# One-hot gate matrix in bf16, tokens innermost, gates in three bf16 parts

## The chip, the core and the metric

The kernel runs on one core of a Trainium2 chip. The metric is device time in microseconds (us), lower is better; the kernel before took 3196.64 us (median of 3 runs, 3196.23 to 3197.21). Engines are named as in the profile: PE multiplies matrices (PEld is its weight load), DVE is the vector engine, ACT the activation engine, POOL issues the gathers, SP most other DMAs.

## The reference

One decoder block over 512 tokens of width 2048: a mixer (pooling and latent attention), a PEER expert layer, a gated embedding and a final norm, in float32. The change touches only the PEER layer. For each token and each of 8 heads it picks 16 of 128 x 128 experts and gives each a softmax gate:

```python
best_v, best_pos = lax.top_k(cand_v, PEER_TOPK)          # 16 of 256 pairs, per head
expert = jnp.take_along_axis(cand_id, best_pos, axis=-1) # i * 128 + j
gate = jax.nn.softmax(best_v, axis=-1)
hc = einsum('cd,chkd->chk', xc, u[ec]);  ac = gc * gelu(hc);  out = einsum('chk,chkd->cd', ac, v[ec])
```

## The kernel before

For 352 of the tokens the kernel doesn't gather experts. It computes the scores of all 16384 experts with dense products, multiplies them by a gate matrix G that is zero where an expert wasn't picked, and multiplies by all of v. For a token t, G[j, i] is the sum over its 128 picks (8 heads x 16) of gate x onehot(j) x onehot(i). The first 128 of these tokens get G by scattered DMA adds. The other 224 get it from matrix products, and this is the stage that changes, called the one-hot stage below.

The 224 tokens are 7 blocks of 32 (`ONE_TB`), and a block is 4 groups of 8 tokens (`OH`): 28 groups. The picks lie on the 128 partitions. Per group:

- DVE compares the numbers i and j of the picks with the row 0..127 (`iota`) and gets `one_ij`, 2 x 8 x 128 float32 (L1713), then multiplies the one-hot of i by the gate and gets `one_g`, 8 x 128 float32 (L1717). The number 0..127 is innermost in both. The buffers alternate, so group q waits for the products of group q-2.
- PE multiplies, per token, the one-hot of j (stationary, 128 x 128) with `one_g` (moving, 128 columns): 8 products in float32 into two PSUM banks (L828). The profile has two records for each float32 product, 16 in a group.
- ACT copies both banks into `g_blk`, with the tokens innermost there (L1196). After 4 groups SP stores the block.

Between the groups PE does a dense product of its own, with weights that are split into a high and a low part: unit by unit, each in 4 quarters of 12 matmuls (L533 to L535, 352 columns, float32r). The order on PE in a block is quarter, group, quarter, group, and so on. ACT makes the high part of the next unit's weights in two halves (`w_hi`, L949), between the copies of a block's first, second and third group. DVE makes the low part (`w_lo`, L1350) from it: the half 0 after the one-hots of the second group, the half 1 after those of the third. SP loads the next weights once a half of `w_lo` is done. DVE also takes dot products with gathered rows (`row_dot`, L1689): two in block 0, one behind each of the blocks 1, 2 and 4. POOL issues the gathers and waits for these.

Ahead of the stage, PE turns the picked i, j and gates into token columns, ACT copies them to `hk_t` (L1171), and then ACT issues 8 small DMAs and goes on with the next weights.

Of the kernel before, what the change touches and what calls it, by code (L numbers as in the profile page):

```python
# [8 lines left out]
BF16 = mybir.dt.bfloat16  # L9
U32 = mybir.dt.uint32  # L10
I32 = mybir.dt.int32
ALU = mybir.AluOpType
ACT = mybir.ActivationFunctionType
AX = mybir.AxisListType

P = 128
# [12 lines left out]
NK = 128  # L29
HK = PH * TOPK  # L30
TD = 352
TCD = TD // P + 1
# [41 lines left out]
OH = 8  # L74
# [10 lines left out]
def build_block(nc, x_t, p_t, positions, gains, consts, rope_cols, pool_inv, w_in, pool_w, w_head, w_v,  # L85
                w_o, w_q, keys, u_t, u_rows, v, w_proj, w_gate, out_t):
    ctx = ExitStack()
    with ctx:
# [4 lines left out]
        def at(name, offset, shape, dtype=F32):  # L93
            return nc.alloc_sbuf_tensor_at(name, shape, dtype, offset=base + offset)

        K = 1024
# [5 lines left out]
        h_at, one, two, rest = 40 * K, 72 * K, 136 * K, 200 * K  # L102
# [10 lines left out]
        iota = at("iota", rest + 512, [P, P])  # L113
# [73 lines left out]
        b_inv = at("b_inv", one + 52 * K + 320, [P, TC])  # L187
        t_if = [at(f"t_if{i}", one + 53 * K + 256 * i, [P, TC, TOPK]) for i in range(2)]

        hk_t = at("hk_t", one, [P, 3, TCD * P])  # L190
        one_ij = [at(f"one_ij{i}", one + (6 + 8 * i) * K, [P, 2, OH, NK]) for i in range(2)]
        one_g = [at(f"one_g{i}", one + (22 + 4 * i) * K, [P, OH, NK]) for i in range(2)]
        g_blk = [at(f"g_blk{i}", one + (30 + 16 * i) * K, [P, NK, TB]) for i in range(2)]

        h_out = at("h_out", one + 62 * K, [P, TD])
# [25 lines left out]
        bank = [ctx.enter_context(nc.psum_tensor(f"bank{i}", [P, T], F32)) for i in range(8)]  # L221

        def sem(name):
            return ctx.enter_context(nc.semaphore(name))
# [70 lines left out]
        gates_put = sem("gates_put")  # L295
        hk_turned = sem("hk_turned")
        hk_ready = sem("hk_ready")
        oh_g = sem("oh_g")
        oh_ij = sem("oh_ij")
        g_done = sem("g_done")  # L300
# [59 lines left out]
        def row_loads(k):  # L360

            return k // 2 + 1 if k < EARLY else (k - EARLY) // 4 + 1 + (EARLY // 2 if k % 4 < 2 else 0)
# [167 lines left out]
        def _(pe):  # L530
# [280 lines left out]
            for i in range(3):  # L811
                for t in range(1, TCD):
                    mm = pe.transpose(bank[i][:, t * P:(t + 1) * P],
                                      sel[i][:, t, :, :].rearrange("p h k -> p (h k)"), ident[:, :])
# [4 lines left out]
            def g_group(q, s, first=False):  # L819

                pe.wait_ge(oh_g, q + 1)
                for half in range(2):
                    out = bank[6 + half]
                    if not first:
                        pe.wait_ge(g_out, 2 * q - 1 + half)
                    for t in range(4):
                        o = 4 * half + t
                        mm = pe.matmul(out[:, t * P:(t + 1) * P], one_ij[s][:, 1, o, :], one_g[s][:, o, :],  # L828
                                       start=True, stop=True)
                    mm.then_inc(g_done, 1)  # L830

            def g_block(b, k):
# [82 lines left out]
            for n in range(DC):  # L915
# [7 lines left out]
                for c in range(2):  # L923
                    mm = passes(bank[n % 4][:, :], b + c, u % 2, pt_hi[:, c, :], pt_lo[:, c, :], c == 0, c == 1)
# [17 lines left out]
        def _(act):  # L942
# [206 lines left out]
            for e in range(ALONE):  # L1149
                hi(U_ALONE + e + 1, (U_ALONE + e + 1) % 2)  # L1150
                if e < 2:
                    rows_stage(4 * e)
                    rows_stage(4 * e + 1)
                if e == 2:
                    act.wait_ge(col_made, 1)
                    act.activation(rinv_col[:, :], bank[2][:, 0:4], ACT.Copy).then_inc(col_made, 1)
                if e == 3:
                    gates(PH - 1)
                spill(2 * (PH - 1) + e, e % 2, U_ALONE + e)
                if e < 2:  # L1160
                    rows_stage(4 * e + 2)
                    rows_stage(4 * e + 3)
                    rows_evict(2 * e)
                    rows_evict(2 * e + 1)
                if e == 1:
                    act.activation(stage[0][:, 0, :].rearrange("p (q t) -> p q t", t=TK),
                                   rinv[:, TD:TD + TK].unsqueeze(1).to_broadcast([P, 4, TK]), ACT.Copy).then_inc(stage_ready, 1)
                if e == 5:
                    for i in range(3):
                        act.wait_ge(hk_turned, i + 1)  # L1170
                        act.activation(hk_t[:, i, P:TCD * P], bank[i][:, P:TCD * P], ACT.Copy).then_inc(hk_ready, 1)  # L1171
                    act.wait_ge(topk_step, PER_TOPK * PH)
                    for q in range(4):
                        ts = slice(TK * q, TK * (q + 1))
                        act.dma_start(expert_b[ts, :], expert_c[P - TK:P, 2 * q:2 * q + 2, :].rearrange("p a k -> p (a k)"))\
                           .then_inc(expert_b_in, 16)
                        act.dma_start(gate_rows_b[ts, :],
                                      sel[2][P - TK:P, TCD - 1, 2 * q:2 * q + 2, :].rearrange("p a k -> p (a k)"))\
                           .then_inc(expert_b_in, 16)
# [165 lines left out]
        def _(dve):  # L1345
            def lo(u, slot, halves=(0, 1), n=8):

                for s in halves:
                    dve.wait_ge(hi_ready, 2 * u + s + 1)
                    dve.tensor_tensor(w_lo[slot][:, 8 * s:8 * s + n, :], raw[s][:, 0:n, :],  # L1350
                                      w_hi[slot][:, 8 * s:8 * s + n, :].bitcast(F32), ALU.subtract)\
                       .then_inc(lo_ready, 1)
# [333 lines left out]
            def row_dot(k, b, loads, part_b=False):  # L1686

                dve.wait_ge(row_in[b], 16 * loads)
                dve.scalar_tensor_tensor(row[b][:, :], row[b][:, :], 1.0, (x_rows_b if part_b else x_rows)[:, :],  # L1689
                                         ALU.mult, ALU.mult,  # L1690
                                         accum_out=column(dots_b if part_b else dots, k)).then_inc(row_done, 1)
# [9 lines left out]
            dve.wait_ge(rows_out, 4)  # L1701
            for k in range(2):
                row_dot(k, k % 2, row_loads(k))
            for n in range(6):
                lo(U_ALONE + 7 + n, (U_ALONE + 1 + n) % 2)
                for k in ((2,), (3, 4), (5,), (6, 7), (8,), (9, 10))[n]:
                    row_dot(k, k % 2, row_loads(k))

            def one_hots(q, s, first=False):
                o = [P, 2, OH, NK]  # L1710
                if not first:
                    dve.wait_ge(g_done, 2 * q - 2)
                dve.tensor_tensor(one_ij[s][:, :, :, :], iota[:, None, None, :].to_broadcast(o),  # L1713
                                  hk_t[:, 0:2, bass.ds(OH * q + P, OH)].unsqueeze(3).to_broadcast(o), ALU.is_equal)\
                   .then_inc(oh_ij, 1)
                dve.wait_ge(oh_ij, q + 1)
                dve.tensor_tensor(one_g[s][:, :, :], one_ij[s][:, 0, :, :],  # L1717
                                  hk_t[:, 2, bass.ds(OH * q + P, OH)].unsqueeze(2).to_broadcast([P, OH, NK]), ALU.mult)\
                   .then_inc(oh_g, 1)

            dve.wait_ge(hk_ready, 3)

            BLOCK_DOT = {1: 13, 2: 14, 4: 15}

# [447 lines left out]
```

## Time and profile before

| | us |
|---|---|
| median of 3 runs | 3196.64 |
| the profiled execution | 3193.13 |
| its span | 3190.9 |
| PE busy | 3069.8 |
| DVE busy | 2493.5 |
| ACT busy | 1053.9 |

The profile is one execution. "Busy" is the time in which an engine has an instruction in work. A busy PE isn't at its peak, as the ends of matmuls are modelled; the distance from one start to the next shows its pace. A line such as L828 is that of the kernel before.

### The profile page before, as it was taken

To read this page: it belongs to the slowest core of one execution; us is meant where nothing else is said; L and a number is where in the kernel's file an instruction comes from. 1 tells how busy PE (TensorE), PEld (TensorE's weight loads), DVE (VectorE), ACT (ScalarE), POOL (GpSimd) and SP (SyncE) were. 2 spreads that over 40 slices of the span, in tenths; PEclk is the share of its full clock that TensorE was granted. 3 is DMA by queue.
4 is the path that set the end of the run, shared out by engine and by line. 5 is a ranking of instruction groups with operands and counts; after the bars stand their busy time and mean duration, and the time that the engine had idled before them with its cause. 6 is when DMAs were issued, how large, how long until landed. Compare 5 with 4: busy or idle time off the path is not lost.

```text
span 3190.9 us, 47109 instructions
## 1 busy us (share of the span) xinstructions
PE 3069.8 (96%) x17044; PEld 2843.0 (89%) x17044; DVE 2493.5 (78%) x3559; ACT 1053.9 (33%) x1409; POOL 815.3 (26%) x530
## 2 busy tenths in 40 slices
PE   7999999999998879999999999999999999999997
PEld 5777778788888779999999999999999999999775
DVE  6444444499996979999999998999999999966545
ACT  4223433222233543333333333333333333324322
POOL 3030000046675112222222223232323232302000
PEclk8999999999999999999999999999999999999998
DMA  3233222344558669999999998999999999953222
GB/s 142 93 135 115 79 80 92 105 112 105 114 146 275 221 255 336 358 346 337 348 334 350 333 352 319 340 344 339 344 337 348 335 351 339 346 188 113 93 92 92
DMA packets 254755, 756.37 MB, mean 237 GB/s; under 512 B 37216, under 2 KB 90976, under 8 KB 210656
## 3 DMA queue, kind: packets, MB, share of 16 engines
q1 hardware_dynamic: 185184, 414.05, 38.0%
q0 software_dynamic: 64512, 335.64, 28.0%
q10 hardware_dynamic: 4992, 5.80, 0.5%
q8 instruction: 41, 0.67, 0.1%
q14 instruction: 26, 0.21, 0.0%
HBM read 722.28 MB, written 33.10 MB: 237 GB/s over the span
## 4 chain that ended last, share of the span: by engine, by line
PE 76%; DVE 16%; DMA 3%; issue 3%; ACT 1%; POOL 1%; DVEq 0%; ACTq 0%; SPq 0%; POOLq 0%
PE bank L533 24%; PE bank L535 24%; PE bank L534 23%; DVE w_lo L1350 3%; DVE row L1689 2%; DVE one_ij L1713 1%; DMA raw<-in_v 1%; PE bank L625 1%; PE bank L648 1%; PE bank L626 1%; DVE w_lo L1362 1%; DMA row<-in_u_rows,expert 1%; DVE one_g L1717 1%; DVE x_lo L1870 1%; PE bank L828 1%
## 5 line engine op out<-in xcount | busy, mean ns | idle before, releaser
L533 PE MATMUL bank<-x_hi,w_hi 128*128 128x352 f32 (+1 forms) x3024 | 1073.8, 355 | 30.9 <-DVE x_lo L1378 16.6
L535 PE MATMUL bank<-x_hi,w_lo 128*128 128x352 f32 (+1 forms) x3024 | 1063.7, 352 | 0.0
L534 PE MATMUL bank<-x_lo,w_hi 128*128 128x352 f32 (+1 forms) x3024 | 1057.6, 350 | 0.0
L533 PE MATMUL bank<-a_hi,w_hi 128*128 128x352 f32 x2048 | 664.8, 325 | 11.6 <-DVE a_lo L1764 8.2
L534 PE MATMUL bank<-a_lo,w_hi 128*128 128x352 f32 x2048 | 664.1, 324 | 0.0
L535 PE MATMUL bank<-a_hi,w_lo 128*128 128x352 f32 x2048 | 664.1, 324 | 0.0
L533 PEld LDWEIGHTS bank<-x_hi,w_hi 128*128 128x128 f32 x3024 | 573.4, 190 | 86.1 <-DVE w_lo L1350 16.8
L535 PEld LDWEIGHTS bank<-x_hi,w_lo 128*128 128x128 f32 x3024 | 573.4, 190 | 44.0
L534 PEld LDWEIGHTS bank<-x_lo,w_hi 128*128 128x128 f32 x3024 | 573.8, 190 | 43.1 <-issue 1.2
L533 PEld LDWEIGHTS bank<-a_hi,w_hi 128*128 128x128 f32 x2048 | 387.6, 189 | 14.1 <-DVE a_lo L1764 7.3
L534 PEld LDWEIGHTS bank<-a_lo,w_hi 128*128 128x128 f32 x2048 | 387.7, 189 | 0.0
L535 PEld LDWEIGHTS bank<-a_hi,w_lo 128*128 128x128 f32 x2048 | 387.7, 189 | 0.0
L961 ACT ACTIVATE w_hi<-raw 128x1024 fp32r<-128x1024 f32 x216 | 223.1, 1053 | 435.2 <-PE bank L535 424.2
L961 ACT ACTIVATE w_hi<-raw_b 128x1024 fp32r<-128x1024 f32 x216 | 223.3, 1053 | 418.5 <-PE bank L535 410.0
L2050 POOL DMA_INDIRECT row<-in_v,expert x128 | 231.9, 1812 | 476.5 <-DVE x_rows L1698 391.7
L2050 POOL DMA_INDIRECT row<-in_u_rows,expert x128 | 200.0, 1563 | 586.8 <-DVE row L1689 534.4
L1350 DVE TENSOR_TENSOR w_lo<-raw,w_hi 128x1024 fp32r<-128x1024 f32 (+1 forms) x236 | 278.6, 1213 | 80.8 <-ACT w_hi L949 74.6
L1838 DVE TENSOR_TENSOR h<-bank,h 128x352 f32<-128x352 f32 x512 | 257.0, 517 | 83.8 <-PE bank L535 83.7
L2032 POOL DMA_INDIRECT gate_matrix<-put_gate,cell x128 | 229.3, 1791 | 358.8 <-DVE cell L1647 300.8
L1698 DVE SCALAR_TENSOR_TENSOR x_rows<-row,mix,x_rows 128x2048 f32<-128x2048 f32 x128 | 299.9, 2343 | 6.6 <-DMA row<-in_v,expert 6.6
L949 ACT ACTIVATE w_hi<-raw 128x1024 fp32r<-128x1024 f32 (+1 forms) x236 | 235.9, 1031 | 201.7 <-PE bank L535 67.0
L1689 DVE SCALAR_TENSOR_TENSOR row<-row,x_rows 128x2048 f32<-128x2048 f32 x128 | 292.0, 2282 | 8.6 <-DMA row<-in_u_rows,expert 8.6
(221 smaller groups left out, 2894.8 us busy)
## 6 DMA issues: line engine op xcount, KB each, us to landing
raw<-in_u_t SPq DMA_DIRECT2D x164, 512.0 KB
raw<-in_v SPq DMA_DIRECT2D x132, 512.0 KB
raw_b<-in_v SPq DMA_DIRECT2D x124, 512.0 KB
raw_b<-in_u_t SPq DMA_DIRECT2D x92, 512.0 KB
g_tile<-gate_matrix SPq DMA_DIRECT2D x32, 704.0 KB
raw<-in_w_o SPq DMA_DIRECT2D x32, 512.0 KB
raw<-in_w_q SPq DMA_DIRECT2D x32, 512.0 KB
raw<-in_w_gate SPq DMA_DIRECT2D x32, 512.0 KB
```

Of the source, the lines that this page charges most:

```text
L533: pe.matmul(out, w_hi[slot][:, blk, :], m_hi, start=first, stop=False)
L534: pe.matmul(out, w_hi[slot][:, blk, :], m_lo, start=False, stop=False)
L535: return pe.matmul(out, w_lo[slot][:, blk, :], m_hi, start=False, stop=last)
L625: pe.matmul(out[:, 0:n], q_n[:, ts], k_n[:, 0:n], start=True, stop=False)
L949: act.activation(w_hi[slot][:, 8 * s:8 * s + n, :], raw[s][:, 0:n, :], ACT.Copy)\
L961: act.activation(w_hi[slot][:, 8 * s:8 * s + 8, :], raw_two[x][s][:, :, :], ACT.Copy).then_inc(hi_ready, 1)
L1350: dve.tensor_tensor(w_lo[slot][:, 8 * s:8 * s + n, :], raw[s][:, 0:n, :], w_hi[slot][:, 8 * s:8 * s + n, :].bitcast(F32), ALU.subtract)\
L1689: dve.scalar_tensor_tensor(row[b][:, :], row[b][:, :], 1.0, (x_rows_b if part_b else x_rows)[:, :], ALU.mult, ALU.mult, accum_out=column(d ...
L1698: dve.scalar_tensor_tensor(to[:, :], row[b][:, :], column(mix_b if part_b else mix, k), to[:, :], ALU.mult, ALU.add).then_inc(row_done, 1)
L1838: dve.tensor_tensor(hc, bank[2 + c][:, 0:TD], hc, ALU.add).then_inc(v_added, 1)
L2032: pool.indirect_dma_start(g_dram.rearrange("b j i t -> (b j i t)").unsqueeze(1), bass.IndirectOffsetOnAxis(ap=cell[:, hd, k:k + 1], axis=0 ...
L2050: pool.indirect_dma_start(row[b][:, :], None, table, bass.IndirectOffsetOnAxis(ap=index, axis=0))\
```

## The change

`hk_t` becomes three tensors: i and j in bf16 (`hk_ij`), the gate in float32 (`hk_gate`) and the gate in three bf16 parts (`hk_g`). ACT writes the first part and also a bf16 table `iota_oh` of 128 x 8 numbers, in which each number stands 8 times. DVE takes each part from the gate and rounds the rest to the next part (`split_gates`), ahead of the fourth of six weight units. `one_ij` and `one_g` are bf16 with the 8 tokens innermost, and `one_g` has three parts: 3 x 128 x 8 elements. Each product per token becomes three bf16 products into the same place, and both operands of a product are read at a step of 8 elements, 16 bytes. The numbers 0 to 127 and the ones are exact in bf16.

```diff
--- before.py
+++ after.py
@@ -187,9 +187,12 @@
         b_inv = at("b_inv", one + 52 * K + 320, [P, TC])
         t_if = [at(f"t_if{i}", one + 53 * K + 256 * i, [P, TC, TOPK]) for i in range(2)]
 
-        hk_t = at("hk_t", one, [P, 3, TCD * P])
-        one_ij = [at(f"one_ij{i}", one + (6 + 8 * i) * K, [P, 2, OH, NK]) for i in range(2)]
-        one_g = [at(f"one_g{i}", one + (22 + 4 * i) * K, [P, OH, NK]) for i in range(2)]
+        hk_ij = at("hk_ij", one, [P, 2, TCD * P], BF16)
+        hk_g = at("hk_g", one + 2 * K, [P, 3, TCD * P], BF16)
+        hk_gate = at("hk_gate", one + 28 * K, [P, TCD * P])
+        one_ij = [at(f"one_ij{i}", one + (6 + 4 * i) * K, [P, 2, NK, OH], BF16) for i in range(2)]
+        one_g = [at(f"one_g{i}", one + (14 + 6 * i) * K, [P, 3, NK, OH], BF16) for i in range(2)]
+        iota_oh = at("iota_oh", one + 26 * K, [P, NK, OH], BF16)
         g_blk = [at(f"g_blk{i}", one + (30 + 16 * i) * K, [P, NK, TB]) for i in range(2)]
 
         h_out = at("h_out", one + 62 * K, [P, TD])
@@ -295,6 +298,7 @@
         gates_put = sem("gates_put")
         hk_turned = sem("hk_turned")
         hk_ready = sem("hk_ready")
+        hk_split = sem("hk_split")
         oh_g = sem("oh_g")
         oh_ij = sem("oh_ij")
         g_done = sem("g_done")
@@ -825,8 +829,9 @@
                         pe.wait_ge(g_out, 2 * q - 1 + half)
                     for t in range(4):
                         o = 4 * half + t
-                        mm = pe.matmul(out[:, t * P:(t + 1) * P], one_ij[s][:, 1, o, :], one_g[s][:, o, :],
-                                       start=True, stop=True)
+                        for part in range(3):
+                            mm = pe.matmul(out[:, t * P:(t + 1) * P], one_ij[s][:, 1, :, o], one_g[s][:, part, :, o],
+                                           start=part == 0, stop=part == 2)
                     mm.then_inc(g_done, 1)
 
             def g_block(b, k):
@@ -1168,7 +1173,11 @@
                 if e == 5:
                     for i in range(3):
                         act.wait_ge(hk_turned, i + 1)
-                        act.activation(hk_t[:, i, P:TCD * P], bank[i][:, P:TCD * P], ACT.Copy).then_inc(hk_ready, 1)
+                        act.activation(hk_ij[:, i, P:TCD * P] if i < 2 else hk_gate[:, P:TCD * P], bank[i][:, P:TCD * P],
+                                       ACT.Copy).then_inc(hk_ready, 1)
+                    act.activation(hk_g[:, 0, P:TCD * P], bank[2][:, P:TCD * P], ACT.Copy).then_inc(hk_ready, 1)
+                    act.activation(iota_oh[:, :, :], iota[:, :].unsqueeze(2).to_broadcast([P, NK, OH]), ACT.Copy)\
+                       .then_inc(hk_ready, 1)
                     act.wait_ge(topk_step, PER_TOPK * PH)
                     for q in range(4):
                         ts = slice(TK * q, TK * (q + 1))
@@ -1701,24 +1710,36 @@
             dve.wait_ge(rows_out, 4)
             for k in range(2):
                 row_dot(k, k % 2, row_loads(k))
+
+            def split_gates():
+
+                rest_of = hk_gate[:, P:TCD * P]
+                dve.wait_ge(hk_ready, 4)
+                for part in range(2):
+                    dve.tensor_tensor(rest_of, rest_of, hk_g[:, part, P:TCD * P], ALU.subtract).then_inc(hk_split, 1)
+                    dve.wait_ge(hk_split, 2 * part + 1)
+                    dve.tensor_copy(hk_g[:, part + 1, P:TCD * P], rest_of).then_inc(hk_split, 1)
+                    dve.wait_ge(hk_split, 2 * part + 2)
+
             for n in range(6):
+                if n == 3:
+                    split_gates()
                 lo(U_ALONE + 7 + n, (U_ALONE + 1 + n) % 2)
                 for k in ((2,), (3, 4), (5,), (6, 7), (8,), (9, 10))[n]:
                     row_dot(k, k % 2, row_loads(k))
 
             def one_hots(q, s, first=False):
-                o = [P, 2, OH, NK]
+                o, o3 = [P, 2, NK, OH], [P, 3, NK, OH]
+                ts = bass.ds(OH * q + P, OH)
                 if not first:
                     dve.wait_ge(g_done, 2 * q - 2)
-                dve.tensor_tensor(one_ij[s][:, :, :, :], iota[:, None, None, :].to_broadcast(o),
-                                  hk_t[:, 0:2, bass.ds(OH * q + P, OH)].unsqueeze(3).to_broadcast(o), ALU.is_equal)\
-                   .then_inc(oh_ij, 1)
+                dve.tensor_tensor(one_ij[s][:, :, :, :], iota_oh[:, None, :, :].to_broadcast(o),
+                                  hk_ij[:, :, ts].unsqueeze(2).to_broadcast(o), ALU.is_equal).then_inc(oh_ij, 1)
                 dve.wait_ge(oh_ij, q + 1)
-                dve.tensor_tensor(one_g[s][:, :, :], one_ij[s][:, 0, :, :],
-                                  hk_t[:, 2, bass.ds(OH * q + P, OH)].unsqueeze(2).to_broadcast([P, OH, NK]), ALU.mult)\
-                   .then_inc(oh_g, 1)
-
-            dve.wait_ge(hk_ready, 3)
+                dve.tensor_tensor(one_g[s][:, :, :, :], one_ij[s][:, 0:1, :, :].to_broadcast(o3),
+                                  hk_g[:, :, ts].unsqueeze(2).to_broadcast(o3), ALU.mult).then_inc(oh_g, 1)
+
+            dve.wait_ge(hk_ready, 5)
 
             BLOCK_DOT = {1: 13, 2: 14, 4: 15}
```

## Rows read from the trace of the kernel before

**Rows 1.** The page: span, and busy time of the engines.

```profile
span 3190.9 us, 47109 instructions
...
PE 3069.8 (96%) x17044; PEld 2843.0 (89%) x17044; DVE 2493.5 (78%) x3559; ACT 1053.9 (33%) x1409; POOL 815.3 (26%) x530
```

**Rows 2.** The chain that ended last, into the one-hot stage: start us, us, what.

```profile
974.32 1.24 DVE w_lo L1350
...
1027.75 3.79 PE bank L828 x16
```

**Rows 3.** Groups, 1024 to 1160 us: xcount | busy us, mean ns | idle before, releaser.

```profile
L1713 DVE TENSOR_TENSOR one_ij<-iota,hk_t 128x2048 f32<-128x2048 f32 x28 | 64.0, 2286 | 0.0
L828 PE MATMUL bank<-one_g,one_ij 128*128 128x128 f32 x448 | 58.1, 284 | 29.7 <-DVE one_g L1717 29.7
L1196 ACT ACTIVATE g_blk<-bank 128x512 f32<-128x512 f32 x56 | 57.4, 1122 | 61.7 <-PE bank L828 61.7
...
L1717 DVE TENSOR_TENSOR one_g<-one_ij,hk_t 128x1024 f32<-128x1024 f32 x28 | 34.3, 1225 | 1.0
```

**Rows 4.** Busy time of each engine in one block, with the granted clock.

```profile
1072.00:1091.00 19.00, 15.62 (x112) 14.75 (x112) 18.10 (x13) 10.18 (x12) 2.77 (x1) 1.00 0.59 218
```

**Rows 5.** DVE in order of time: start us, us, what [idle before].

```profile
1088.10 1.23 DVE L1717 TENSOR_TENSOR one_g<-one_ij,hk_t 128x1024 f32<-128x1024 f32 x1
...
1093.57 1.23 DVE L1350 TENSOR_TENSOR w_lo<-raw,w_hi 128x1024 fp32r<-128x1024 f32 x1 [0.78 <-ACT w_hi L949]
```

**Rows 6.** PE in order of time, blocks 2 to 6: start us, us, what.

```profile
1070.28 2.05 PE L828 MATMUL bank<-one_g,one_ij 128*128 128x128 f32 x16 [1.74 <-DVE one_g L1717]
...
1089.46 2.05 PE L828 MATMUL bank<-one_g,one_ij 128*128 128x128 f32 x16 [1.66 <-DVE one_g L1717]
...
1106.84 1.95 PE L828 MATMUL bank<-one_g,one_ij 128*128 128x128 f32 x16
...
1108.54 0.41 PE L533 MATMUL bank<-x_hi,w_hi 128*128 128x352 f32 x1
...
1110.60 1.95 PE L828 MATMUL bank<-one_g,one_ij 128*128 128x128 f32 x16
...
1156.72 2.05 PE L828 MATMUL bank<-one_g,one_ij 128*128 128x128 f32 x16 [0.56 <-DVE one_g L1717]
```

**Rows 7.** PE in order of time, matmuls of 512 and 352 columns.

```profile
253.61 0.40 PE L533 MATMUL bank<-l_hi,w_hi 128*128 128x512 f32 x1
...
257.72 0.39 PE L533 MATMUL bank<-l_hi,w_hi 128*128 128x512 f32 x1
...
1095.60 0.33 PE L533 MATMUL bank<-x_hi,w_hi 128*128 128x352 f32 x1
...
1096.58 0.33 PE L533 MATMUL bank<-x_hi,w_hi 128*128 128x352 f32 x1
```

**Rows 8.** Groups of the whole span: a strided read, a dense read, dense writes.

```profile
L1386 DVE TENSOR_REDUCE fold<-ident 128x32 f32<-128x128 f32 x1 | 0.4, 367 | 0.0
...
L1621 DVE TENSOR_REDUCE b_sum<-b_exp 128x4 f32<-128x64 f32 x8 | 1.8, 220 | 0.3
...
L1018 ACT ACTIVATE q_n<-bank 128x512 f32<-128x512 f32 x12 | 7.2, 598 | 6.7 <-PE bank L535 6.6
...
L1109 ACT ACTIVATE h_out<-bank 128x352 f32<-128x352 f32 x32 | 14.8, 461 | 58.0 <-PE bank L535 55.2 <-DMA spilled_scores<-h_out 2.8
```

**Rows 9.** Groups of the whole span: DVE with two tensor operands and with one.

```profile
L1408 DVE TENSOR_TENSOR ang<-ang,turn 128x512 f32<-128x512 f32 x1 | 0.7, 691 | 0.0
...
L1402 DVE TENSOR_SCALAR turn<-ang 128x512 f32<-128x512 f32 x1 | 0.4, 428 | 0.0
```

**Rows 10.** ACT and DVE in order of time, ahead of the stage.

```profile
973.23 2.00 ACT L949 ACTIVATE w_hi<-raw 128x1024 fp32r<-128x1024 f32 x2 [5.03 <-issue]
...
989.66 2.35 DVE L1350 TENSOR_TENSOR w_lo<-raw,w_hi 128x1024 fp32r<-128x1024 f32 x2
995.29 2.29 DVE L1689 SCALAR_TENSOR_TENSOR row<-row,x_rows 128x2048 f32<-128x2048 f32 x1 [3.27 <-DMA row<-in_u_rows,expert]
```

## The prediction

> **What bounds the kernel now.** I read the page first: PE is busy 3069.8 of 3190.9 us [rows 1], so nearly everything elsewhere hides behind PE, and a change counts only where PE waits or where PE's own work grows. The chain of waits enters the one-hot stage through DVE's weight split and leaves DVE at the first group of products, at 1027.75 us [rows 2]; from there it runs over DVE's one-hots in every block. The groups of the stretch say the same: between 1024 and 1160 us PE is idle 29.7 us ahead of its products, all of it for `one_g`, while ACT is idle 61.7 us for PE [rows 3]. DVE is busy 18.10 of 19 us in a block, PE 15.62, at full granted clock (2.4 GHz) [rows 4]. The last group starts at 1156.72 us and takes 2.05 [rows 6], so the stage, from the first product to the last, is 1158.77 - 1027.75 = 131.0 us.
>
> PE's own part: the group that starts at 1106.84 is followed by a dense quarter at 1108.54 and that by a group at 1110.60 [rows 6]. So a group is 1.70 us of PE and a quarter 2.06, together 3.76, 15.0 for a block of four. A block takes 1106.84 - 1089.46 = 17.4 us without a row dot and 1089.46 - 1070.28 = 19.2 with one [rows 6]. The 2 to 4 us between are what DVE costs, and all that the change can save there.
>
> **DVE's one-hots.** 1024 elements take 1.225 us and 2048 take 2.286 [rows 3]: 1.036 ns each and 0.164 fixed. Now `one_ij` has 2048 and `one_g` 3072 elements. At the old pace per element that is 2.29 + 3.35 us; at two elements a cycle 1.22 + 1.75. The trace has no bf16 operation with two tensors. It has DVE at twice its pace with one tensor: 512 elements take 0.428 us, against 0.691 with two [rows 9]. So the bounds of a group are 2.97 and 5.64 us, against 3.51 now. I take 2.97: all operands are 16 bits wide and dense innermost. The Trainium skill, VectorE: DVE Perf Modes, "The perf-mode tier table", gives a bf16 `tensor_tensor` from SBUF twice the rate; no run here shows it yet, and the value taken agrees with it.
>
> **PE's products.** This is the term that decides. There are 24 bf16 matmuls of 128 columns in a group in place of 16 float32 records in 1.70 us. If the reads don't matter, their pace comes from the dense rows: 18 steps of 512 columns in 257.72 - 253.61 = 4.11 us are 228 ns each, 6 steps of 352 in 0.98 us are 163 ns [rows 7]. That is 0.406 ns a column (one a cycle of 2.4 GHz) and 20 ns fixed, so 72 ns at 128 columns and 24 x 72 = 1.73 us a group: no saving on PE, and no loss.
>
> But both operands are now read at a step of 16 bytes, where before their elements were neighbours. Two rows show an access with such a jump. ACT's copy into `g_blk` writes 512 elements at a jump of 128 bytes: 57.4 / 56 = 1.025 us, against 0.598 for a dense write of as many [rows 3, 8]. Dense, 352 elements take 0.461, so an element is 0.137 / 160 = 0.86 ns and 0.16 is fixed, and the strided write costs (1.025 - 0.16) / 512 = 1.69 ns an element, twice as much. DVE's `fold` reads 128 elements at a jump of 128 bytes in 0.367 us; a dense reduction of 64 takes 0.220, of which 64 x 1.036 ns are work and 0.154 fixed, so the strided read costs (0.367 - 0.154) / 128 = 1.67 ns an element [rows 8]. Two engines whose dense paces differ (0.86 and 1.04 ns) pay the same 1.67 ns per jump: that looks like the memory, not the engine. If PE pays it too, a matmul of 128 columns takes 128 x 1.67 = 213 ns, and a group 24 x 213 = 5.12 us. Dense float32r reading at one column a cycle needs 16 bytes in 1.67 ns, so nothing in the trace shows PE reaching more of the memory than that. The bounds of a group on PE are then 1.3 us (24 x 128 columns at 2.4 GHz, nothing fixed) and 5.6 (the 20 ns added to 213). I take 5.12, by the two rows with a jump.
>
> The Trainium skill, Advanced Engine Details and Errata, "SBUF Cachelines", speaks against the layout too: lines of 16 bytes, and at least two hits on a line are needed to absorb the access latency. A step of 16 bytes gives one hit. The two rows agree that jumps cost. The page states no price for PE. The Trainium skill's other page on it, SBUF — State Buffer, "Door 1: The DMA port swizzle", calls a stride of 8 bf16 elements free; by that the sum would be that of the first rival, and the rows as they stand speak against it.
>
> **The sum.** With 5.12 us a group, PE is the bound of the stage: 4 x (5.12 + 2.06) = 28.7 us a block, while DVE needs 4 x 2.97 + 2 x 1.23 = 14.3 (24 even at the slow bound) and ACT 10.2 as now [rows 4]. PE never waits after the first group, so the stage is 28 x 5.12 + 27 x 2.06 = 143.4 + 55.6 = 199.0 us, against 131.0: +68.0. The idle time of 29.7 us is swallowed by this. The five row dots and `w_lo` hide behind PE.
>
> Ahead of the stage ACT gets two more instructions in front of its 8 DMA issues and of the `w_hi` at 973.23 [rows 10]: a copy of 256 elements from PSUM (about 0.27 us behind another) and `iota_oh`, 1024 elements, about 1.0. DVE waits for that `w_hi` and its `w_lo` at 974.32 is in the chain [rows 2], so +1.2. The four DVE steps of `split_gates`, 256 elements each, are at most 4 x (0.164 + 0.267) = 1.7 us, ahead of the `w_lo` at 989.66. DVE then waits 3.27 us for a gathered row [rows 10], which covers them; what isn't covered is the weight load that this `w_lo` releases, so 0 to 1.7, and I take 0.5. The first one-hots are 0.5 shorter. Together +1.2, between -0.5 and +3.
>
> Behind the stage the last copies, the store of `gate_matrix` and the wait for it are as before: 0.
>
> Total +68.0 + 1.2 = +69. The profiled execution has 3193.13 us, its span of 3190.9 and 2.2 around it; that gives 3262. It lies 3.5 us under the median of the runs, so against the median the forecast is 3196.64 + 69 = 3266 us. With 233 ns a matmul it is 28 x 5.59 + 55.6 = 212, +82, 3279.
>
> **Rival 1: PE reads at full pace, faster.** For it: before, nothing is strided on PE, so no row shows a price there; one line holds what eight bf16 columns need if it is kept. Against it: the two rows with jumps. Then a group is 1.73 us on PE and DVE's order decides. From the start of a block's first group to the first `w_lo` there are 1093.57 - 1089.46 = 4.1 us (products, copies, `w_hi`) [rows 5, 6]; then `w_lo` 1.15, one-hots 2.94, `w_lo` 1.14, one-hots 2.94: the fourth group starts at 12.3. Its products and a quarter (1.73 + 2.06) bring the next block to 16.1, against 17.4; with a row dot, one-hots (2.94) and dot (2.2) behind 12.3 give 17.4, against 19.2. Three blocks save 1.3, three 1.8, block 0 about 2: 11.3. Less 1.2 ahead: -10, 3186 us; 3184 at 56 ns a matmul.
>
> **Rival 2: PE reads at half pace.** A price of one cycle of 1.2 GHz per jump is 107 ns a matmul. For it: PE takes two columns in that time when dense, so its port may be wider than DVE's. A group is 2.56 us, the stage 28 x 2.56 + 55.6 = 127.3, less than 131.0: -3.7 + 1.2 = -2.5, 3194 us. With the fixed 20 ns it is 3.05 a group, 141.0, +11, 3208. The point from which this turns slower is 2.7 us a group.
>
> **Rival 3: PE's clock falls as well.** With products at a quarter of their pace PE streams less, and the clock does fall here: behind the idle wait ahead of the stage the first group took 3.79 us, the later ones about 2 [rows 2, 6]. If it fell to 1.2 GHz through the stage, each quarter would take 4.1: 27 x 2.06 = 55 more, 3321 us. Against it: the dense quarters still stream 2.06 us of every 7.2.
>
> **Rival 4: DVE doesn't pair elements**, with PE at full pace. 5.6 us a group: a block is 4 x 5.55 + 2.3 = 24.5, the stage 7 x 24.5 + 11 for the dots = 182, about +50: 3247 us. Against it: the operands are dense and 16 bits wide, and DVE does pair elements with one tensor [rows 9].
>
> **How the numbers follow.** Chances: forecast (PE at 213 to 233 ns) 0.44, rival 1 0.25, rival 2 0.22, rival 3 0.05, rival 4 0.04. A difference under 0.2% (6.4 us) can't be told from none. Faster is rival 1 but for its edge, 0.23. The same are that edge and over half of rival 2, 0.14. Slower is the rest, 0.63. For 8 in 10 the range must take in rival 1, rival 2 and the forecast with its higher pace: 3184 to 3285. The forecast's own range is 3258 to 3285.
>
> **What would show it.** Right: the start of a bf16 matmul in the products lies 200 to 235 ns behind the one before; a block is about 29 us; PE has no idle time for `one_g` after the first group and DVE has plenty. `one_ij` takes 1.22 us and `one_g` 1.75 (wrong if 2.3 and 3.3). The first product starts 0 to 3 us after 1027.75. Wrong: matmuls 55 to 80 ns apart with blocks of 16 to 17 us (rival 1), or 107 to 130 apart with blocks of 18 to 20 (rival 2); a granted clock of about 0.5 in the stage (rival 3).

## The result, and the profile after

The changed kernel took 3315.88 us (median of 4 runs, 3310.97 to 3316.97), the kernel before 3196.93 us on the same chip (3196.23 to 3201.55). The ratio is 1.037, with a 95% interval of 1.0354 to 1.0385: it is slower by 119 us. The forecast was 3266 us with a range to 3285. The sign and the place were right, and 50 us were missing.

The page of the kernel after, its span, the busy time of the engines, and the clock granted to PE in 40 slices of the span. It answers to [rows 1].

```profile
span 3314.7 us, 47564 instructions
...
PE 3211.4 (97%) x17268; PEld 2928.2 (88%) x17268; DVE 2482.6 (75%) x3563; ACT 1059.4 (32%) x1411; POOL 809.1 (24%) x530
...
PEclk9999999999997677999999999999999999999998
```

The span grew by 3314.7 - 3190.9 = 123.8 us and PE's busy time by 141.6. DVE's fell by 11. The four slices of 7, 6, 7 and 7 are the one-hot stage. Before, all slices but the first and the last had 9.

Groups of the stage after, 1028 to 1280 us, columns as in [rows 3]:

```profile
L833 PE MATMUL bank<-one_g,one_ij 128*128 128x128 bf16 x672 | 162.8, 415 | 9.5 <-DVE one_g L1739 9.5
...
L1739 DVE TENSOR_TENSOR one_g<-one_ij,hk_g 128x3072 bf16<-128x3072 bf16 x28 | 49.2, 1759 | 1.0
...
L1736 DVE TENSOR_TENSOR one_ij<-iota_oh,hk_ij 128x2048 bf16<-128x2048 bf16 x28 | 34.2, 1222 | 43.1 <-PE bank L833 43.1
...
L1359 DVE TENSOR_TENSOR w_lo<-raw,w_hi 128x1024 fp32r<-128x1024 f32 x14 | 17.2, 1226 | 84.4 <-ACT w_hi L954 84.4
```

Set beside [rows 3], the roles have changed. DVE's two operations fell from 2286 + 1225 ns to 1222 + 1759 = 2981 ns a group, and DVE is now idle ahead of `one_ij` (43.1 us) and of its weight split (84.4 us). PE waited 29.7 us for `one_g` before, 8.6 of it ahead of the first group. It now waits 9.5, all of it ahead of the first group. Its products went from 58.1 to 162.8 us of busy time.

Three stretches of the stage after. Columns: start:end and length in us, busy us (and instructions) of PE, PEld, DVE, ACT and POOL, granted PE clock, share of the DMA engines, GB/s. They answer to [rows 4].

```profile
1066.00:1102.00 36.00, 36.00 (x145) 27.13 (x144) 16.16 (x13) 10.96 (x11) 0.99 (x1) 0.64 0.31 117
1102.00:1137.00 35.00, 35.00 (x145) 26.27 (x144) 16.06 (x13) 10.91 (x11) 1.97 (x1) 0.74 0.32 123
1173.00:1209.00 36.00, 36.00 (x145) 27.11 (x144) 16.41 (x13) 11.05 (x11) 4.15 (x3) 0.69 0.33 119
```

A block now takes 35 to 36 us of PE without a gap, where 17.4 to 19.2 went by before and the prediction had 28.7. PE is busy 36.00 of 36 us and yet has only 0.64 of its full clock.

PE in order of time, in the kernel after: start us, us, what.

```profile
1030.94 5.81 PE L833 MATMUL bank<-one_g,one_ij 128*128 128x128 bf16 x24 [9.53 <-DVE one_g L1739]
...
1084.97 5.82 PE L833 MATMUL bank<-one_g,one_ij 128*128 128x128 bf16 x24
1090.43 0.66 PE L537 MATMUL bank<-x_hi,w_hi 128*128 128x352 f32 x1
1090.89 0.49 PE L538 MATMUL bank<-x_lo,w_hi 128*128 128x352 f32 x1
1091.18 0.49 PE L539 MATMUL bank<-x_hi,w_lo 128*128 128x352 f32 x1
...
1094.12 5.84 PE L833 MATMUL bank<-one_g,one_ij 128*128 128x128 bf16 x24
...
1272.75 5.81 PE L833 MATMUL bank<-one_g,one_ij 128*128 128x128 bf16 x24
1283.35 0.47 PE L539 MATMUL bank<-x_hi,w_lo 128*128 128x352 f32 x1
1283.64 0.34 PE L537 MATMUL bank<-x_hi,w_hi 128*128 128x352 f32 x1
```

Two sizes are to be read here. A group holds PE from 1084.97 to 1090.43: 5.46 us, which is 227 ns for each of 24 matmuls in the mean. The quarter behind it, the same float32r matmuls as before, starts them 1091.18 - 1090.89 = 0.29 us apart, where the rows before had 0.163. For 352 columns that is 1.2 GHz in place of 2.4, and this quarter takes 1094.12 - 1090.43 = 3.69 us. At the end one sees the clock come back: at 1283.64 us, 5.1 us after the last group ended, a matmul's record falls from 0.49 to 0.34.

Where the 123.8 us are, from these rows. From the first product to the end of the last the stage takes 1278.56 - 1030.94 = 247.6 us (1278.56 is the end of the last group's record, 1272.75 + 5.81), against 131.0: +116.6. In it:
- groups: 28 x (5.46 - 1.70) = +105.3;
- quarters: (247.6 - 28 x 5.46) / 27 = 3.51 us in the mean in place of 2.06, so 27 x 1.45 = +39.2;
- PE's idle time and its first group at a low clock, in the stage before: -(131.0 - 28 x 1.70 - 27 x 2.06) = -27.8.

The first product starts 3.2 us later (1030.94 against 1027.75), and what follows the stage takes 4.0 us more. 116.6 + 3.2 + 4.0 = 123.8.

### The profile page after: what moved, and what is told of

Same layout as the page of the kernel before. It is cut to its first block, busy times and chain, and to the rows that moved or that the text cites. A ratio compares the mean times of both kernels' runs of the same rounds, so it can differ in the third digit from the quotient of the medians.

```text
span 3314.7 us, 47564 instructions
## 1 busy us (share of the span) xinstructions
PE 3211.4 (97%) x17268; PEld 2928.2 (88%) x17268; DVE 2482.6 (75%) x3563; ACT 1059.4 (32%) x1411; POOL 809.1 (24%) x530
## 4 chain that ended last, share of the span: by engine, by line
PE 80%; DVE 13%; DMA 3%; issue 2%; ACT 1%; DVEq 0%; ACTq 0%; POOL 0%; SPq 0%; POOLq 0%
PE bank L537 24%; PE bank L539 24%; PE bank L538 23%; PE bank L833 5%; DVE w_lo L1359 2%; DVE row L1698 1%; DMA raw<-in_v 1%; PE bank L629 1%; DMA raw<-in_u_t 1%; PE bank L652 1%; PE bank L630 1%; DVE w_lo L1371 1%; DVE x_lo L1891 1%; DVE x_lo L1387 1%; DVE h L1859 1%
## 5 line engine op out<-in xcount | busy, mean ns | idle before, releaser
L537 PE MATMUL bank<-x_hi,w_hi 128*128 128x352 f32 (+1 forms) x3024 | 1092.3, 361 | 34.6 <-DVE x_lo L1387 19.2
L539 PE MATMUL bank<-x_hi,w_lo 128*128 128x352 f32 (+1 forms) x3024 | 1079.5, 357 | 0.0
L538 PE MATMUL bank<-x_lo,w_hi 128*128 128x352 f32 (+1 forms) x3024 | 1073.7, 355 | 0.0
L537 PEld LDWEIGHTS bank<-x_hi,w_hi 128*128 128x128 f32 x3024 | 587.8, 194 | 90.9 <-DVE w_lo L1359 18.6
L539 PEld LDWEIGHTS bank<-x_hi,w_lo 128*128 128x128 f32 x3024 | 586.9, 194 | 43.9
L538 PEld LDWEIGHTS bank<-x_lo,w_hi 128*128 128x128 f32 x3024 | 587.5, 194 | 43.0 <-issue 1.2
```

The source lines that it names most:

```text
L537: pe.matmul(out, w_hi[slot][:, blk, :], m_hi, start=first, stop=False)
L538: pe.matmul(out, w_hi[slot][:, blk, :], m_lo, start=False, stop=False)
L539: return pe.matmul(out, w_lo[slot][:, blk, :], m_hi, start=False, stop=last)
```

## Experiments

The forecast's theory was that PE pays for every 16-byte line that an operand's read touches, by a price of the memory. After the result there were four questions. Is it the step of the reads? Which of the two operands? Is the lower clock due to it as well, or to the bf16 matmuls as such? And is DVE's saving to be had without PE's loss?

### Dense reads on PE, all else as changed

```diff
+ij_flat = one_ij[s][:, 1, :, :].rearrange("p n o -> p (n o)")
 for part in range(3):
-    mm = pe.matmul(out[:, t * P:(t + 1) * P], one_ij[s][:, 1, :, o], one_g[s][:, part, :, o],
+    g_flat = one_g[s][:, part, :, :].rearrange("p n o -> p (n o)")
+    mm = pe.matmul(out[:, t * P:(t + 1) * P], ij_flat[:, o * P:(o + 1) * P], g_flat[:, o * P:(o + 1) * P],
...
```

> The changed kernel, but each bf16 product reads both operands as 128 neighbouring elements of the same tiles (the values are others, so the gate matrix is left wrong). DVE, ACT and the counts are untouched. Theory (the 16-byte step sets PE's pace, and the slow products let the clock fall): matmuls 72 ns apart (55 to 80), 1.73 us a group, granted clock 1.0 in the stage, blocks of 16 to 17.5 us, total 3189 us (3183 to 3195), so slightly faster than before or the same. Rival (the three-fold count of bf16 products is the cost, not the step): matmuls stay near 227 ns apart and the time near 3316. Second rival (the clock falls for another reason): products 72 to 110 ns apart but quarters still 3.5 us, total about 3230.

This kernel leaves the gate matrix wrong. It took 3187.01 us (9 runs, 3177.92 to 3190.26), a ratio to the kernel before of 0.9963 [0.995, 0.9976]. The same stage, in PE's order of time and as a window:

```profile
1049.36 1.51 PE L835 MATMUL bank<-one_g,one_ij 128*128 128x128 bf16 x24 [2.73 <-DVE one_g L1741]
1050.68 0.41 PE L537 MATMUL bank<-x_hi,w_hi 128*128 128x352 f32 x1
```

```profile
1060.00:1090.00 30.00, 23.74 (x248) 22.15 (x249) 28.75 (x22) 16.80 (x19) 3.43 (x2) 1.00 0.63 238
```

The same 672 matmuls, the same bytes in the tiles and the same work on DVE; only the step is 1 element in place of 8. A group takes 1.32 us (55 ns a matmul) in place of 5.46, the clock is 1.00, and 129 us are gone. So the whole loss, PE's pace and the clock, comes from the strided reads. This is the kernel that the prediction's first rival described (3186 us), with the pace that it lacked.

### Four steps side by side

The eight token pairs of a group read both operands at 1, 2, 4 and 8 elements (2, 4, 8 and 16 bytes), two pairs each.

```diff
+def at_step(flat, k):
+    first = o % k + (o // k) * P * k
+    return flat[:, first:first + P * k - k + 1:k] if k > 1 else flat[:, first:first + P]
...
+if o in (0, 1):
+    mm = pe.matmul(to, at_step(ij_flat, 1), at_step(g_flat, 1), **ends)
+elif o in (2, 3):
+    mm = pe.matmul(to, at_step(ij_flat, 2), at_step(g_flat, 2), **ends)
...
```

> The changed kernel, but within each group of 8 tokens the first two are read by PE at a step of 1 element in both operands, the next two at 2, then 4, then 8 (other values, so the gate matrix is left wrong). Theory A (each 16-byte line costs 1.67 ns whatever is taken from it): per matmul 72 ns at step 1, 60 to 72 at step 2, 107 to 125 at step 4, 227 at step 8. Theory B (a cliff: only a step of a whole line costs): 72, 72, 72, 227. A group is 2.9 us by A, 2.7 by B; total 3200 to 3225 depending on the clock.

One run, 3204.09 us. One group; the four lines are the four steps, six matmuls each:

```profile
1082.08 0.51 PE L843 MATMUL bank<-one_g,one_ij 128*128 128x128 bf16 x6
1082.42 0.51 PE L845 MATMUL bank<-one_g,one_ij 128*128 128x128 bf16 x6
1082.77 0.88 PE L847 MATMUL bank<-one_g,one_ij 128*128 128x128 bf16 x6
1083.46 1.58 PE L849 MATMUL bank<-one_g,one_ij 128*128 128x128 bf16 x6
1084.68 0.53 PE L537 MATMUL bank<-x_hi,w_hi 128*128 128x352 f32 x1
```

From start to start six matmuls take 0.34, 0.35, 0.69 and 1.22 us: 57, 58, 115 and 203 ns each. The last figure is low, because the dense matmul behind a strided stretch starts before the last strided one has had its full share; a whole group of 24 at that step gave 227. Steps of 1 and 2 elements cost the same, 4 elements cost twice that, 8 elements four times. So each 16-byte line costs about 1.8 ns (64 lines in 115 ns, 128 in 227), and where a line holds enough columns the one column a cycle of 2.4 GHz is the limit. No step above 8 elements was run, so that the price stays at one line's there isn't shown for PE. The Trainium skill, Advanced Engine Details and Errata, "SBUF Cachelines", says that at least two hits on a line are needed to absorb the latency. For PE's bf16 operands two aren't enough in this run: with two hits (step 4) a matmul takes 115 ns against 57 dense, and with four (step 2) 58.

### Which operand

```diff
+if o in (0, 1):
+    mm = pe.matmul(to, at_step(ij_flat, 1), at_step(g_flat, 8), **ends)
+elif o in (2, 3):
+    mm = pe.matmul(to, at_step(ij_flat, 8), at_step(g_flat, 1), **ends)
...
```

The other two quarters of the pairs read both dense, and both at 8.

> The changed kernel, but within each group of 8 tokens two are read with only the moving operand at a step of 8 elements, two with only the stationary, two with both dense, two with both at a step of 8 (other values, so the gate matrix is left wrong). Theory: the moving operand sets the pace: 227, 72, 72, 227 ns a matmul. Rival: the weight load pays too and isn't hidden: 227, 150 to 230, 72, and 227 or more. If the two add up, both strided would be slower than moving alone.

One run, 3219.10 us. One group, in that order:

```profile
1087.78 1.53 PE L843 MATMUL bank<-one_g,one_ij 128*128 128x128 bf16 x6
1089.13 0.55 PE L845 MATMUL bank<-one_g,one_ij 128*128 128x128 bf16 x6
1089.52 0.50 PE L847 MATMUL bank<-one_g,one_ij 128*128 128x128 bf16 x6
1089.85 1.55 PE L849 MATMUL bank<-one_g,one_ij 128*128 128x128 bf16 x6
1091.04 0.52 PE L537 MATMUL bank<-x_hi,w_hi 128*128 128x352 f32 x1
```

```profile
1090.00:1130.00 40.00, 40.00 (x264) 31.17 (x263) 28.13 (x21) 20.50 (x21) 1.70 (x1) 1.00 0.50 191
```

A strided moving operand (`one_g`, in the second place here) takes 1.35 us for six, 225 ns each. A strided stationary operand (`one_ij`, the weight load) takes 0.39 us, 65 ns, against 55 with both dense. So the moving operand sets nearly the whole price, and the weight load at the same step costs 10 ns. The theory had 72 ns for each of the two.

This bears on the prediction's reason. The strided weight load touches the same 128 lines, and it keeps up with a matmul every 65 ns: 0.5 ns a line at most. So 1.7 ns isn't what the memory asks of every reader. On PE it belongs to the read of the moving operand.

The window has PE reading half of its products at the slow pace, busy throughout, with the clock at 1.00. It isn't so in the whole stage. A window and PE's order of time further on:

```profile
1130.00:1180.00 50.00, 50.00 (x323) 39.10 (x323) 33.98 (x26) 24.83 (x25) 6.42 (x3) 0.97 0.44 162
```

```profile
1156.35 0.66 PE L537 MATMUL bank<-x_hi,w_hi 128*128 128x352 f32 x1
...
1160.03 1.53 PE L843 MATMUL bank<-one_g,one_ij 128*128 128x128 bf16 x6
```

One quarter, from 1156.35 to 1160.03 us, ran at 1.2 GHz and took 3.68 us, with no idle time of PE ahead of it.

### One product in place of three

This kernel leaves out two of the three bf16 parts of each gate.

```diff
-for part in range(3):
-    mm = pe.matmul(out[:, t * P:(t + 1) * P], one_ij[s][:, 1, :, o], one_g[s][:, part, :, o],
-                   start=part == 0, stop=part == 2)
+mm = pe.matmul(out[:, t * P:(t + 1) * P], one_ij[s][:, 1, :, o], one_g[s][:, 0, :, o],
+               start=True, stop=True)
```

> The changed kernel with only the first of the three bf16 products per token (two thirds of the products left out, so gates are rounded), operands still at a step of 8 elements: 8 slow matmuls in a group, 8 x 227 ns = 1.82 us. Theory (the clock falls because slow products fill over half of PE's time): here they fill under half, the granted clock stays near 1.0 and the quarters at 2.06 us; total 3190 (3185 to 3200). Rival (strided products lower the clock however few they are): quarters 3.5 us, 28 x 1.82 + 27 x 3.5 = 145 us for the stage, total about 3214.

3191.26 us (8 runs), ratio 0.9982 [0.9971, 0.9992]. Two windows of its stage:

```profile
1049.00:1066.00 17.00, 16.59 (x74) 13.73 (x73) 12.02 (x10) 8.70 (x10) 0.00 (x0) 0.77 0.51 193
1084.00:1101.00 17.00, 16.48 (x85) 12.96 (x84) 15.56 (x13) 10.88 (x12) 1.70 (x1) 1.00 0.73 258
```

PE in order of time, a group at the low clock and one at the full clock:

```profile
1051.58 2.08 PE L832 MATMUL bank<-one_g,one_ij 128*128 128x128 bf16 x8
1053.29 0.66 PE L537 MATMUL bank<-x_hi,w_hi 128*128 128x352 f32 x1
...
1056.90 2.06 PE L832 MATMUL bank<-one_g,one_ij 128*128 128x128 bf16 x8
1058.60 0.53 PE L537 MATMUL bank<-x_hi,w_hi 128*128 128x352 f32 x1
```

Eight strided matmuls take 1.71 us of PE at the low clock and 1.70 at the full one, as long as the 16 float32 records did [rows 6]. So the low clock doesn't slow the strided reads; it slows the dense quarters, here to 3.61 us (1056.90 - 1053.29). And 16 more strided matmuls, as in the changed kernel's group, cost 5.46 - 1.71 = 3.75 us, 234 ns each: that is their pace from start to start, and 227 is the mean of a group, whose last matmul holds up the dense one behind it by less.

The total came as the theory had it, the clock only in part. Of seven windows of 17 or 18 us over the stage two have 1.00, three 0.91 and the first two 0.78 and 0.77. Nor does the time in strided reads order the runs: the run before had more of it, 1.35 + 1.19 us of each group and quarter of about 5.4, against 1.7 of about 3.9 here, and behind the first groups it lost its clock in one quarter only. What brings the fall isn't settled by these two.

### As much PE time, but dense

Is the clock lower because of the strided reads, or because a group of bf16 matmuls lasts over 5 us? This kernel computes every dense product four times over.

```diff
-for part in range(3):
+for part in (0, 1, 2) * 4:
```

> Dense reads as in e1_dense, with each of the 24 products of a group issued four times (other values): 96 dense matmuls of 57 ns are 5.4 us a group, as long as the 24 strided ones. Theory (the clock falls because PE streams few columns while it reads at a step): here PE streams all the time, the granted clock stays at 1.0, quarters take 2.06 us, the stage is 28 x 5.4 + 27 x 2.06 = 207 us, total 3276 us (3268 to 3284), 40 us under the changed kernel. Rival (the clock falls because of long bf16 groups between float32r quarters, whatever their reads): quarters 3.5 us, total 3316.

3286.30 us (2 runs), ratio 1.0273 [1.0255, 1.0292]. PE in order of time, and a window:

```profile
1080.41 5.53 PE L835 MATMUL bank<-one_g,one_ij 128*128 128x128 bf16 x96
1085.75 0.41 PE L537 MATMUL bank<-x_hi,w_hi 128*128 128x352 f32 x1
...
1087.81 5.53 PE L835 MATMUL bank<-one_g,one_ij 128*128 128x128 bf16 x96
...
1155.59 0.42 PE L537 MATMUL bank<-x_hi,w_hi 128*128 128x352 f32 x1 [2.99 <-issue]
...
1162.73 7.97 PE L835 MATMUL bank<-one_g,one_ij 128*128 128x128 bf16 x96 [4.92 <-issue]
```

```profile
1060.00:1090.00 30.00, 30.00 (x442) 29.46 (x440) 16.56 (x13) 10.90 (x11) 1.73 (x1) 1.00 0.34 120
```

A group takes 5.34 us, within 2% of the 5.46 of the changed kernel, and the quarter behind it 2.06 (1087.81 - 1085.75), with the clock at 1.00. So it is the strided reading, not the length or the kind of the groups, that takes the clock. Whether the clock follows the jumps themselves or only the slow pace that they give PE, no run separates: this one changes both. The kernel is 30 us faster than the changed one, although its groups take nearly as long: that difference is the quarters at the lower clock. It is some 10 us over the 3276 that were expected, and the last two rows hold these: two stops of PE with no releaser, 2.99 and 4.92 us, and one group of 7.97 us in place of 5.53, 10.3 in all. Why PE stopped there isn't known. The other execution (3284.24 us) is over the 3276 too, by 8 us, so something of the kind may belong to this kernel; that execution has no profile.

### Two tokens innermost

PE pays nothing for a step of 2 elements, and DVE may need no more than two neighbours innermost. So the tiles get the two tokens of a pair innermost, in place of eight. Nothing is left out.

```diff
-one_ij = [at(f"one_ij{i}", one + (6 + 4 * i) * K, [P, 2, NK, OH], BF16) for i in range(2)]
-one_g = [at(f"one_g{i}", one + (14 + 6 * i) * K, [P, 3, NK, OH], BF16) for i in range(2)]
+one_ij = [at(f"one_ij{i}", one + (6 + 4 * i) * K, [P, OH // 2, 2, NK, 2], BF16) for i in range(2)]
+one_g = [at(f"one_g{i}", one + (14 + 6 * i) * K, [P, OH // 2, 3, NK, 2], BF16) for i in range(2)]
...
-mm = pe.matmul(out[:, t * P:(t + 1) * P], one_ij[s][:, 1, :, o], one_g[s][:, part, :, o],
+mm = pe.matmul(out[:, t * P:(t + 1) * P], one_ij[s][:, o // 2, 1, :, o % 2],
+               one_g[s][:, o // 2, part, :, o % 2],
...
```

`hk_ij`, `hk_g` and `iota_oh` get the same order, and with them the instructions that write and read them.

> The changed kernel with two tokens innermost in place of eight: every bf16 tile is laid out in pairs of tokens, so PE reads at a step of 2 elements (4 bytes) and DVE still finds two 16-bit neighbours. Nothing is left out. Theory (PE's price is per 16-byte line, DVE's double pace wants only neighbours): one_ij 1.22 us, one_g 1.76, matmuls 57 ns apart, a group 1.33 us on PE, granted clock 1.0, blocks of about 15.9 us (17.2 with a row dot), total 3187 us (3183 to 3191), faster than before by 0.3%. Rival (rows of two elements cost DVE its double pace): one_ij 2.3 and one_g 3.3 us, blocks of 25, total about 3245.

3185.08 us (5 runs, 3181.80 to 3188.87), ratio 0.9961 [0.9948, 0.9975]. Groups of its stage, 1024 to 1152 us:

```profile
L1745 DVE TENSOR_TENSOR one_g<-one_ij,hk_g 128x3072 bf16<-128x3072 bf16 x28 | 49.2, 1759 | 1.0
L833 PE MATMUL bank<-one_g,one_ij 128*128 128x128 bf16 x672 | 45.8, 225 | 27.9 <-DVE one_g L1745 27.9
...
L1740 DVE TENSOR_TENSOR one_ij<-iota_oh,hk_ij 128x2048 bf16<-128x2048 bf16 x28 | 34.1, 1219 | 0.0
...
L1362 DVE TENSOR_TENSOR w_lo<-raw,w_hi 128x1024 fp32r<-128x1024 f32 x15 | 18.3, 1222 | 14.9 <-ACT w_hi L955 14.9
```

DVE keeps its doubled pace with rows of two elements (1219 and 1759 ns), and PE's products take 45.8 us, below the 58.1 of [rows 3]. The saving is 0.4%, as with fully dense reads. PE still waits 27.9 us for `one_g`, 9.9 of it ahead of the first group. The last line gives one reason: DVE's `w_lo` waits 14.9 us for ACT's `w_hi`. 5.5 of these lie ahead of the first group, where ACT's `w_hi` waits for its weights; the other 9.4 are waits of 1.0 to 1.8 us in each block, where ACT makes `w_hi` behind the copies of a product.

### `w_hi` ahead of the copies, in both kernels

```diff
+hi(b + U_BLOCK + 1, (U_BLOCK + 1 + s) % 2, halves=(0,))
 g_evict(b, s, 0)
-hi(b + U_BLOCK + 1, (U_BLOCK + 1 + s) % 2, halves=(0,))
 g_evict(b, s, 1)
```

On top of the tokens in pairs:

> The pairs layout, and ACT makes the first half of w_hi before it copies the block's first group, not after. Theory (with dense products DVE waits about 1 us a block for that w_hi, and PE waits for DVE): DVE has no wait left, a block is DVE's 4 x 2.93 + 2.28 = 14.0 us, 16.2 with a row dot; 7 blocks save another 1.0 to 1.9 us each against the pairs alone, total 3177 us (3172 to 3182). Rival (the w_hi was not what DVE waited for, or PE's order gives the time back): as the pairs alone, 3187.

And on the kernel before, alone:

> The kernel before with ACT's order alone changed: the first half of w_hi ahead of the copies of the block's first group. It tells how much of the gain of the pairs with that order is due to the order. Theory: DVE loses its wait of about 1 us in each block, blocks of 16.2 and 18.4 us in place of 17.4 and 19.2, total 3190 us (3187 to 3193). Rival: no change, 3197.

With the pairs it took 3179.18 us (5 runs, 3176.10 to 3185.31), ratio 0.9945 [0.993, 0.996]; on the kernel before 3191.64 us (9 runs), ratio 0.998 [0.997, 0.999]. So the order gives about 0.2% by itself, and the medians would have it give as much on top of the pairs, though the intervals of the two kernels with pairs overlap. The longest waits of the stage in the kernel with both, 1024 to 1140 us: who waited for whom, us in all, times, the longest:

```profile
PE bank L833 <- DVE one_g L1745: 24.5, 11, 11.0
...
DVE w_lo L1362 <- ACT w_hi L955: 10.6, 7, 5.4
```

11.0 and 5.4 of these are the entry into the stage. PE still waits 13.5 us for `one_g` in it, against 18.0 with the pairs alone, and DVE 5.2 us for `w_hi`, against 9.4; the theory had none left of the latter. On the kernel before, the order alone took DVE's waits for `w_hi` in the stage from 7.8 to 2.1 us. By its median this is the fastest kernel of the study, 0.55% under the one before.

## Why the prediction was wrong

Right were, by its steps:
- **The bound.** PE became the bound of the stage, DVE got slack, and PE never waited for `one_g` after the first group.
- **DVE's one-hots.** 2.97 us a group taken, 2.98 measured. Rival 4 (3247 us) is refuted.
- **PE's price per line.** 213 ns a matmul taken, 227 measured in a group's mean, inside the 213 to 233 that stood as its range. The size carried over from a strided read on DVE and a strided write on ACT to PE's moving operand: 1.67, 1.69 and 1.77 ns a line. Rivals 1 and 2 went with it. The reason given, "that looks like the memory, not the engine", isn't borne out: the prediction didn't tell the two operands apart, and the stationary one reads the same lines at 0.5 ns each or less. Why three engines come so near each other isn't shown, so this number was in part luck. The Trainium skill, SBUF — State Buffer, "Door 1: The DMA port swizzle", calls a stride of 8 bf16 elements free; here it is 227 ns against 57 for a matmul, so the measurement decides against it for PE's moving operand.
- **Ahead of the stage, roughly.** +1.2 taken, between -0.5 and +3; +3.2 measured, a little outside.

After, in ACT's and DVE's order of time, ahead of the stage; they answer to [rows 10]:

```profile
969.22 0.38 ACT L1176 ACTIVATE hk_ij<-bank 128x256 bf16<-128x256 f32 x1 [0.42 <-PE bank L817]
...
975.58 2.01 ACT L954 ACTIVATE w_hi<-raw 128x1024 fp32r<-128x1024 f32 x2 [4.20 <-issue]
```

```profile
997.61 2.29 DVE L1698 SCALAR_TENSOR_TENSOR row<-row,x_rows 128x2048 f32<-128x2048 f32 x1 [3.31 <-DMA row<-in_u_rows,expert]
...
999.83 0.42 DVE L1719 TENSOR_TENSOR hk_gate<-hk_gate,hk_g 128x256 f32<-128x256 f32 x1
...
1001.07 0.29 DVE L1721 CAST hk_g<-hk_gate 128x256 bf16<-128x256 f32 x1
1001.63 1.23 DVE L1359 TENSOR_TENSOR w_lo<-raw,w_hi 128x1024 fp32r<-128x1024 f32 x1 [0.26 <-ACT w_hi L954]
```

`w_hi` is 2.35 us later than before, but 1.95 of these were there at the copies of `hk_t`, ahead of any added work; ACT's two instructions added 0.4 where 1.2 was taken. The four steps of `split_gates` stand between a row dot and the `w_lo` at 1001.63. The prediction had them one unit of work too early, ahead of the `w_lo` of [rows 10] and with the wait for the gathered row as cover. The wait for a row lies ahead of them there (3.31 us) and covers nothing. They cost about 0.4 us all the same: the `w_lo` starts 1.73 us after the row dot's end, 1.33 in the kernel before. The 0.5 taken was near, by a wrong place. That leaves about 0.4 us of the 3.2 that isn't traced.

**The step that failed is the quarters' term, 27 x 2.06 = 55.6 us.** It held the dense quarters at the full clock's 2.06 us. They took 3.51 us on average, 27 x 1.45 = 39.2 us more, because the granted clock in the stage fell to 0.64 to 0.74. The prediction had this as rival 3, with 3321 us (3316 measured), and gave it 0.05, since "the dense quarters still stream 2.06 us of every 7.2". That rival had the mechanism, and its number came so near by luck: it had every quarter at 4.1 us, +55, where one wholly at the low clock takes 3.69 and the mean is 3.51; the 16 us that it had too much are nearly what the other terms had too little. The runs showed that dense quarters between the groups don't hold the clock up by themselves: with dense groups of the same length the quarters keep 2.06 us, and with strided groups they don't. The one row in which the clock was seen low [rows 2] stood behind an idle wait. None of the rows before showed a PE that is busy without a gap and loses its clock all the same.

Against the forecast of +69.2 the measured 123.8 us are: the quarters +39.2; 5.46 in place of 5.12 us a group, 28 x 0.34 = +9.5; the start +2.0; behind the stage +4.0, where 0 was taken. The last is in part the clock once more: 5.1 us at half pace behind the last group, in place of some 2.8, so 2.3. The remaining 1.7 us of this stays open; it is within the spread between executions of one kernel.

One slip changes nothing: at its slow bound DVE needs 4 x 5.64 + 2 x 1.23 = 25.0 us a block, not 24, still below the 28.7.

## What to carry to other kernels

Price an operand's layout at each engine that reads it. Tokens innermost halved DVE's time for an element and quadrupled PE's for a column, and PE's share was far the larger: the 16-byte steps cost 105 us in the groups and 39 in the quarters, where DVE's gain could bring at most the 28 us by which the stage had been longer than PE's own work. Then look for the layout that both can live with: PE had no loss at a step of 2 elements and DVE needed no more than 2 elements side by side, and that kernel is 0.4% faster than the one before. And where a change makes PE's work slow without making it idle, add a term for the clock on all the dense work around it: here that term was 39 us, and the forecast had 0.

## What the runs showed of the hardware

- Nearly one price where each element stands in another 16-byte line: 1.67 ns for DVE's strided read, 1.69 for ACT's strided write [rows 8], both worked out from one row at a jump of 128 bytes, and 1.77 for PE's moving operand (227 ns / 128; 1.83 by the 234 from start to start). A bf16 matmul of 128 columns takes 55 to 58 ns at steps of 1 and 2 elements, 115 at 4, 227 at 8. The stationary operand at a step of 8 costs 10 ns, and its 128 lines are read in 65 ns or less.
- The strided reads cost the same at both clocks (eight in 1.71 us at the low one, 1.70 at the full one); dense float32r matmuls of 352 columns go from 0.163 to 0.293 us.
- PE was counted busy 36.00 of 36 us at a granted clock of 0.64; with dense bf16 groups of the same length the clock was 1.00.
- Dense bf16 matmuls of 128 columns follow each other at 55 to 57 ns, less than the 72 that the prediction worked out from float32r rows. Nearly nothing is fixed (128 columns at 2.4 GHz are 53).
- DVE handles two bf16 elements in the time of one when its innermost rows have just two elements (1219 ns for 2048, 1759 for 3072), also where one operand is repeated over the outer dimensions.
